# A decoder block on one core: B's transposes behind four tiles of h, pole operations earlier, the S5 input matrix two chunks later

## What is computed

```python
h = rmsnorm(x, norm1_g) * (1.0 + sc1) + sh1        # sh1, sc1, ...: silu(c) @ w_ada + b_ada
z = h @ w_in
u_conv, u_ssm, gl_conv, gl_ssm = split(z)
y_conv = silu(layernorm(causal depthwise conv of 31 taps over a * sigmoid(gate))) @ conv_proj
# S5: the poles give e = exp(dt * a); B is scaled by (e - 1) / a
bu = u_ssm @ B_bar;  x_t = e * x_{t-1} + bu_t;  y = C x + D u
y_ssm = za * sigmoid(zb),  where za, zb = split(gelu(y) @ w_glu)
x = x + g1 * ((sigmoid(gl_conv) * y_conv + sigmoid(gl_ssm) * y_ssm) @ w_out)
h = rmsnorm(x, norm2_g) * (1.0 + sc2) + sh2
x = x + g2 * ((silu(f_gate) * f_up) @ w_ffn_out);  out = rmsnorm(x, final_g)
```

## Time and profile before

| what | us |
|---|---|
| median of 3 runs | 2675.8 |
| lowest, highest | 2668.9, 2676.42 |
| profiled execution, its own time | 2679.86 |
| its span in the trace | 2678.1 |
| PE busy in the span | 2567.8 (96%) |
| DVE, POOL, ACT busy | 1504.9, 1821.0, 725.4 |

### The profile page before, as it was taken

The page is one execution under the profiler, slowest core; times in us unless marked ns, Lnnn a source line. Parts: engine busy times, 40 slices in busy tenths (PEclk is TensorE's granted clock), DMA queues, the critical chain, the costliest instruction groups (busy, mean ns, idle before and its releaser), DMA issues.

```text
span 2678.1 us, 30702 instructions
## 1 busy us (share of the span) xinstructions
PE 2567.8 (96%) x11675; PEld 2112.9 (79%) x11675; DVE 1504.9 (56%) x1782; ACT 725.4 (27%) x1120; POOL 1821.0 (68%) x1204
## 2 busy tenths in 40 slices
PE   6889999999999899989899999999999999999997
PEld 3778787878888788877788888878888878888886
DVE  4999733986299745987633334463333325544631
ACT  3212321133112321135333345443333322111100
POOL 2656675686776677665687777787777756666664
PEclk8999998999999999999999999999999999999999
DMA  8776347653765348562232232322323256655532
GB/s 266 183 183 187 112 162 153 173 184 103 213 169 183 114 145 203 151 204 87 94 103 87 81 116 73 112 84 71 95 71 95 73 196 205 196 163 181 173 134 71
DMA packets 420026, 378.29 MB, mean 141 GB/s; under 512 B 88024, under 2 KB 326312, under 8 KB 419752
## 3 DMA queue, kind: packets, MB, share of 16 engines
q1 hardware_dynamic: 321440, 299.48, 37.0%
q10 hardware_dynamic: 98440, 76.85, 10.3%
HBM read 312.11 MB, written 55.71 MB: 137 GB/s over the span
## 4 chain that ended last, share of the span: by engine, by line
PE 65%; DVE 25%; DMA 4%; issue 2%; ACT 2%; ACTq 1%; POOL 1%; DVEq 0%; POOLq 0%
PE bank L1546 13%; PE bank L1547 13%; PE bank L1548 13%; DVE bank L753 11%; PE bank L1777 6%; PE bank L1775 6%; PE bank L1776 6%; PE bank L1692 2%; PE bank L1694 2%; PE bank L1693 2%; DVE wst L809 1%; DVE bank L787 1%; DMA hraw<-hid_scratch 1%; DVE wst L789 1%; DMA u<-us_scratch 1%
## 5 line engine op out<-in xcount | busy, mean ns | idle before, releaser
L1845 POOL TENSOR_TENSOR w_lo<-raw,w_hi 128x1024 fp32r<-128x1024 f32 x192 | 484.0, 2521 | 15.4
L1843 POOL CAST w_hi<-raw 128x1024 fp32r<-128x1024 f32 x192 | 213.6, 1113 | 410.5 <-PE bank L1548 322.5
L1546 PE MATMUL bank<-h_hi,w_hi 128*128 128x512 f32 x896 | 354.6, 396 | 8.4 <-ACT sg_c L1185 6.5
L1547 PE MATMUL bank<-h_lo,w_hi 128*128 128x512 f32 x896 | 351.2, 392 | 0.0
L1548 PE MATMUL bank<-h_hi,w_lo 128*128 128x512 f32 x896 | 351.0, 392 | 0.0
L753 DVE SCALAR_TENSOR_TENSOR bank<-uc,cwt,bank 128x512 f32<-128x512 f32 x464 | 328.4, 751 | 8.0
L1868 POOL TENSOR_TENSOR fw_lo<-fsum,fw_hi 128x512 fp32r<-128x512 f32 x176 | 234.0, 1331 | 106.9 <-ACT fw_hi L1336 106.9
L1546 PE MATMUL bank<-xc_hi_T,fw_hi 128*128 128x512 f32 x704 | 276.6, 393 | 8.7 <-DVE tr L937 6.3
L1775 PE MATMUL bank<-ow_hi,hid_hi 128*128 128x512 f32 x704 | 274.7, 390 | 3.6 <-DVE hid_lo L997 3.6
L1548 PE MATMUL bank<-xc_hi_T,fw_lo 128*128 128x512 f32 x704 | 275.1, 391 | 0.0
L1547 PE MATMUL bank<-xc_lo_T,fw_hi 128*128 128x512 f32 x704 | 275.0, 391 | 0.0
(11 more groups left out here) (301 smaller groups left out, 5163.4 us busy)
## 6 DMA issues: line engine op xcount, KB each, us to landing
raw<-in_w_in SPq DMA_DIRECT2D x112, 512.0 KB, 4.7
raw<-in_w_ffn_in SPq DMA_DIRECT2D x66, 512.0 KB, 5.3
raw<-in_w_ffn_out SPq DMA_DIRECT2D x66, 512.0 KB, 4.5
hid_scratch<-tr SPq DMA_DIRECT2D x88, 256.0 KB, 2.5
hraw<-hid_scratch SPq DMA_DIRECT2D x88, 256.0 KB, 3.8
g2b<-in_w_ada SPq DMA_DIRECT2D x64, 256.0 KB, 4.2
ssm_m<-vk_scratch SPq DMA_DIRECT2D x32, 512.0 KB, 4.8
raw<-in_ssm_glu SPq DMA_DIRECT2D x32, 512.0 KB, 3.5
```

Source lines behind the costliest of these rows:

```text
L1546: t.matmul(dst, wh, xh, start=first, stop=False)
L1547: t.matmul(dst, wh, xl, start=False, stop=False)
L1843: g.tensor_copy(hi[:], src[:]).then_inc(hi_done, 1)
L1845: g.tensor_tensor(lo[:], src[:], hi[:].bitcast(F32), ALU.subtract).then_inc(split_done, 1)
```

## The change

Four edits. Nothing is computed in another way, and no instruction is added or dropped.

1. `nat_b` moves to the buffers tr and dt_, and B's 32 transposes move from between `ada1` and `ada3` to behind the transposes of h tile 3.
2. On DVE the first pole operations (L622 to L625 before) and the reduction of `th` move ahead of the wait for PE's `sums`; splits 0 to 4 of h come in a row, then `angles`, then splits 5 to 7.
3. PE's and ACT's `state_matrix` moves behind ug1. DVE does u0 and u1 together, and u2 after four output matrices.
4. ACT issues two kernel stores ahead of each of the four second exchanges, and does gl0 and gl1 ahead of the third and the fourth.

```diff
-        nat_b = early(h_at, tr_at, ...)
+        nat_b = early(tr_at, tr_at + 16384, ...)
...
-                names += conv_in(0) + [f"wt{n}" for n in R(8)] + ["ct0", "ct1"] + conv_in(1, 2, 3)
+                names += conv_in(0, 1) + [f"wt{n}" for n in R(8)] + ["ct0", "ct1"] + conv_in(2, 3)
...
+            dve.wait_ge(*scal.after("pro", "dt"))
+            link(v.tensor_tensor(lg, dt, ar, ALU.mult))
+            link(v.tensor_tensor(jexp[:], ...))
+            link(v.tensor_tensor(th, dt, ai, ALU.mult))
+            reduce_angle(th, th, t0)
             dve.wait_ge(*tensor.after("pro", "sums"))
             link(v.tensor_copy(modrow[:], bank[7][0:4, :]), "modrow")
...
             scale_of(0)
-            dve.wait_ge(*scal.after("pro", "dt"))
-            link(v.tensor_tensor(lg, dt, ar, ALU.mult))
-            link(v.tensor_tensor(jexp[:], ...))
-            link(v.tensor_tensor(th, dt, ai, ALU.mult))
-            h_split("pro", 0)
-            reduce_angle(th, th, t0)
-            h_split("pro", 1)
-            h_split("pro", 2)
+            for k in R(5):
+                h_split("pro", k)
             angles(jarg[:, 0, :, :], jarg[:, 1, :, :], jtmp[:], th, T + 1, "jargs")
-            for k in R(3, KD):
+            for k in R(5, KD):
                 h_split("pro", k)
...
             gated(0, 0)
+            gated(0, 1)
...
             for j in R(4):
                 output_matrix(j)
-            gated(0, 1)
+            gated(0, 2)
             for j in R(4, T + 1):
                 output_matrix(j)
-            gated(0, 2)
...
                 if b == 0:
                     sigmoid_u(0)
+                    sigmoid_u(1)
                     state_matrix()
                     rotation_tables()
...
-                if b == 0:
-                    store_kernel()
-                else:
+                if b:
                     sigmoid_u(2)
+                early_gates = 0 if b else 2
                 for q in R(NQ):
+                    if b == 0:
+                        store_kernel(2 * q, 2 * q + 1)
                     if b and q == 2:
                         sigmoid_u(3)
+                    if b == 0 and q >= 2:
+                        gate(q - 2)
                     act.wait_ge(*vec.after(b, f"sc{q}"))
                     exchange(dt_[q][:], wst[:, q * GQ:(q + 1) * GQ, 0:NC], turned_in[q])
                 act.wait_ge(*vec.after(b, "last"))
                 exchange(ctmp[:], carry[:], carry_in)
-                for i in R(GY[b]):
+                for i in R(early_gates, GY[b]):
                     gate(i)
...
             modulation_rows(1)
-            pe.wait_ge(bx_in, 64)
-            (32 transposes of nat_b, step "bx")
             modulation_rows(3)
...
-            for k in R(KD):
+            for k in R(4):
+                transposes("pro", k)
+            pe.wait_ge(bx_in, 64)
+            (32 transposes of nat_b, step "bx")
+            for k in R(4, KD):
                 transposes("pro", k)
...
                 if b == 0:
-                    conv_input(0)
+                    conv_input(0, 1)
                     state_matrix()
-                    conv_input(1, 2, 3)
+                    conv_input(2, 3)
                     kernel_tiles()
```

More of the change, by code:

```diff
@@ L267, in build @@
             ("iota_f", [P, NC + 1]), ("cx", [P, 2, 4, P]))
-        nat_b = early(h_at, tr_at, ("nat_b0", [G, 2, NST, HG]), ("nat_b1", [G, 2, NST, HG]))
+        nat_b = early(tr_at, tr_at + 16384, ("nat_b0", [G, 2, NST, HG]), ("nat_b1", [G, 2, NST, HG]))
         vm, = early(ync_at, mc_at, ("vm", [P, G, T + 1, HG]))
@@ L331, in pe_steps @@
             return names
-        pe_pro = ["v1", "ada1", "bx", "ada3", "v0", "ada5", "ada7", "sums", "mt"] + h_steps + ["v2"]
+        pe_pro = ["v1", "ada1", "ada3", "v0", "ada5", "ada7", "sums", "mt"] + h_steps[0:4] + ["bx"] + h_steps[4:] + ["v2"]
         pe_mix = [pe_steps(b) for b in R(NB)]
@@ L339, in act_steps @@
             if b == 0:
-                names += ["ug0"] + [f"wt{n}" for n in R(8)] + ["sk", "ck"] + [f"ug{m}" for m in R(1, KC)]
+                names += ["ug0", "ug1"] + [f"wt{n}" for n in R(8)] + ["sk", "ck", "ug2", "ug3"]
                 names += [f"kk{n}" for n in R(8)] + [f"S{q}" for q in R(NQ)]
@@ L613, in _ @@
             qr, qi, nr, den = (sv[:, n, :] for n in R(8, 12))
+            dve.wait_ge(*scal.after("pro", "dt"))
+            link(v.tensor_tensor(lg, dt, ar, ALU.mult))
+            link(v.tensor_tensor(jexp[:], iota_f[:, 0:T + 1].unsqueeze(2).broadcast_to([P, T + 1, G]),
+                                 lg.unsqueeze(1).broadcast_to([P, T + 1, G]), ALU.mult))
+            link(v.tensor_tensor(th, dt, ai, ALU.mult))
+            reduce_angle(th, th, t0)
             dve.wait_ge(*tensor.after("pro", "sums"))
@@ L1117, in kernel_tiles, with store_kernel @@
                         .then_inc(*scal.step(0, f"kk{n}"))
-            def store_kernel():
+            def store_kernel(*steps):
                 act.wait_ge(pro_v, mark["kst"])
                 act.wait_ge(zeros_in, 16)
-                for t in R(T):
+                for t in steps:
                     act.dma_start(vk_d[t * HG:(t + 1) * HG, :, 1, t * HG:],
@@ L1164, in mixers @@
                     sigmoid_u(0)
+                    sigmoid_u(1)
                     state_matrix()
                     rotation_tables()
-                    for m in R(1, KC):
-                        sigmoid_u(m)
+                    sigmoid_u(2)
+                    sigmoid_u(3)
                     kernel_tiles()
@@ L1512, in transposes @@
                 ins.then_inc(*tensor.step(stage, f"h{k}"))
-            for k in R(KD):
+            for k in R(4):
+                transposes("pro", k)
+            pe.wait_ge(bx_in, 64)
+            for n in R(2):
+                turned = bank[4 + n][:].rearrange("p (g h) -> p g h", h=HG)
+                for h in R(HG):
+                    ins = t.transpose(turned[:, :, h], nat_b[n][:, :, :, h].rearrange("g a p -> g (a p)"),
+                                      ident[0:G, 0:G])
+            ins.then_inc(*tensor.step("pro", "bx"))
+            for k in R(4, KD):
                 transposes("pro", k)
```

2 lines of the change are left out of this document (removed).

## The result

| | before | changed |
|---|---|---|
| median, us | 2679.5 (9 runs) | 2691.2 (9 runs, 2685.8 to 2692.7) |
| profiled execution, its time | 2679.86 | 2691.32 |
| its span | 2678.1 | 2689.5 |

The ratio is 1.0040, 95% interval 1.0023 to 1.0057: slower by 0.4%, with an interval clear of no change. The forecast was 2681.4 with a range up to 2689. Nine runs of the kernel before now have a median of 2679.5, where the prediction stood on three with 2675.8.

A forecast was written before the change was run, and what follows sets the result against it. The prediction took DVE to bound the changed stretch, almost without a gap from about 61.7 to 272 us. Its terms, -3.3 + 7.6 + 1.3 = +5.6 us on a median of 2675.8, gave 2681.4, range 2670 to 2689.

The forecast's parts named there:

- B's transposes: Start of block 0: slab 3's matmuls start earlier, so slab 7 lands sooner; -3.3 us, bounds -2.5 and -4.3.
- Pole operations: DVE around scale and the poles: little was on the path and later operations go at POOL's pace; 0.
- Kargs: Small operations and kargs on DVE, now beside POOL's chunks 8 and 9: +7.6 us, bounds +4.1 and 0.
- The walk: Operation-by-operation count of DVE's waits for POOL in the kargs stretch: sum 7.9 us, less 0.3 idle anyway, +7.6.
- The rival in which POOL pays in DVE's stead: In kargs the waits fall on POOL, which has time; 2672.5 to 2677, middle 2674 us; chance 0.23.
- ug2: After u0, ua2 starts at a low clock, so DVE waits for ug2's sigmoid; +1.3 us, up to +2.4.
- Scan: Block 0's scan, with kernel tiles and S0 to S3 on TensorE beside DVE's taps: 0.
- Stores and gates, turn back: ACT's spread stores and early gates fit between scans, and POOL has no split in DVE's turn back: 0.
- the rivals, at 0.13 and at 5 us: POOL's splits of chunks 18 and 19 fall into DVE's turn back; +5.6 + 5, about 2687 us; chance 0.13.
- a turn back over 13 us: Sign in block 0 that POOL's splits fall into DVE's turn back, which took 10.85 us before.
- the wait at 272: TensorE's 7.1 us wait for DVE's split of ys at the mixer's end, taking up the 6.5 us saved earlier.
- Sum: All terms together: -3.3 + 7.6 + 1.3 = +5.6 us, from the median 2675.8 to 2681.4.

The follow-up runs named there:

- e_poles: The kernel before with only the early pole operations, th reduction and reordered splits of h; u0 0.4 us later, no difference in time.
- e_hold: The changed kernel with POOL's split of chunk 8 in block 0 held until DVE's kargs is done; kargs stretch 14.60 us, block 1 3.5 us sooner.
- e_pieces89: The changed kernel with POOL's modulation pieces of chunks 8 and 9 put behind chunk 12; kargs stretch 20.18 us, block 1 0.2 us sooner.
- gates alone: The kernel before with gl0 and gl1 ahead of ACT's third and fourth exchange, stores in one row; turn 18.99 us, block 1 at 405.5.
- both: The kernel before with stores in pairs and gl0 and gl1 early; turn 15.93 us, block 1 at 401.6, no difference in time told.
- e_gates_late: The changed kernel with gl0 and gl1 behind all exchanges again, stores still in pairs; 2686.6 us, turn 14.21.
- e_fix: The kernel before with the changed prologue, POOL's pieces moved off poles and kargs, chunk 8's split held until kargs is done; 2668.9 us, ratio 0.9973.
- e_prologue: The kernel before with the moved B transposes and the early pole operations; two series, 2673.3 us against 2678.9 and 2673.6 against 2678.7.

## Why the prediction was wrong, step by step

- **B's transposes, -3.3.** Right. Slab 3's matmuls began at 22.50 and took 5.04 us, slab 7 landed at 33.64, 3.9 us sooner, scale was done at 42.73. The bounds were the clock's, and other executions with this edit lie between them or just below: the first small operation of kargs came 2.3 to 3.8 us sooner.
- **Pole operations, 0.** Right (`e_poles`: u0 +0.4, time the same). In the changed kernel the reduction of th met the split of chunk 0 and TensorE waited 1.9 us for modrow; scale was done 3.8 us sooner all the same.
- **Kargs, +7.6.** Right: 22.17 - 14.59 = 7.58, and 6.9 in the second execution. The walk was right not only in its sum. Operation by operation DVE lost 0.77, 2.08, 1.03, 0.72, 2.05 and 0.94 us, where the walk had nothing, 2.1, 1.25, 0.9, 2.4 and 1.28; taking all of POOL away took everything. The Trainium skill, SBUF — State Buffer, section "Who interferes with whom", has it that a DVE instruction with two SBUF inputs or in a 2-port mode and a GpSimd instruction that reads SBUF exclude each other for the whole instruction; the rows at 96.17 and 104.07 and `e_hold` agree. The rival in which POOL pays in DVE's stead fell: POOL's three rows from 100.28 on were 3.4 us longer as well, but DVE paid its 7.6.
- **ug2, +1.3.** 1.67 in the changed kernel, 1.5 in its second execution, up to 2.8 in others. What the prediction did not say is that this wait stands ready to take back what kargs gives (`e_hold`, `e_pieces89`).
- **Scan, 0.** 26.98 against 26.64.
- **Stores and gates, turn back, 0.** This is the step that failed: the turn back was 3.06 us longer, 3.05 to the first tap. The sentence was "POOL has no split to do in DVE's turn back". The parts were seen rightly: the early gates take away TensorE's stop that had kept POOL out (gates alone: turn 18.99 instead of 13.56), and the late load of chunk 18 had to keep it out in their place (both: 15.93). But I had that load landing near 198, and the turn back ends there as well: a margin of nothing, from a length of SP's loads that I took from no row. The split began at 195.80, some 2.5 us before the 198.4 at which an undisturbed turn back would have ended. The mechanism stood among the rivals, at 0.13 and at 5 us, and by the prediction's own sign, a turn back over 13 us, it is the one that holds. It came at 3 us, since chunk 18's split fell in whole but of chunk 19's only the start. That removing the gates' change gives back 2.4 us of the turn (`e_gates_late`) confirms it. The wait of 6.5 us which went "into the wait at 272" was not neutral.
- **Sum.** Block 0 came out at +8.5, 5.6 of it forecast; the 2.9 left are about the turn back's 3.06. The greater part of the miss is elsewhere. The point stood on a median of three runs, 2675.8, where larger series give 2678.1 to 2679.5. The profiled execution, 2679.86, would have given 2685.5, closer, but that was luck: profiled executions of other kernels here lie up to 7.5 us off their medians. And the first series was some 3 us slower than block 0 explains, which by its median a second one didn't repeat. What these 3 us were is open. With 3.7 for the base, 2.9 for block 0 and 3.2 for the series the miss of 9.8 us is covered.

## What to carry to other kernels

An engine that is on the critical path, and whose operations another engine can hold up as POOL does DVE's here, is protected by that other engine's waits. Before a wait of a third engine (here TensorE at gl4 and ahead of the state matrix) is removed, look up what it holds back, and what runs on the bound engine when that is let go. Put DVE work like kargs, which reads only SBUF, where POOL waits for loads or banks, or hold POOL's next piece with an explicit wait, as `e_hold` and `e_fix` do; but look for the next consumer first, since in `e_hold` holding a split for 15 us made ug2 late. And take as base of a forecast enough runs: the median of three was 3.7 us under that of nine, and a single profiled execution can be further off (`e_fix`: 2662.5 against a median of 2668.9).

## What the runs showed that I had not expected

- A DVE operation on 32 columns took 0.19 us or 2.33 us, by whether an instruction of POOL's split began just ahead of it. One such operation at the end of the carry moved a whole block by 2.1 us between two executions of one kernel.
- TensorE after 7.0 us of waiting: 4.5 us at a mean granted clock of 0.68. After 2.5 us: 1.00. The same matmuls behind it took 1.6 us more, by DVE's idle time until they were done (6.25 us in the kernel before, 4.63 in `e_prologue`). So the bound engine's delay can cost more than itself, and a gain there can bring more. The length of the wait alone does not tell which comes: in the kernel before, a wait of 2.39 us that ended at 1331.10 was followed by a granted clock of 0.50.
- An exchange of 2 times 128 KB took 8.1 us with some 2.5 MB of loads of SP issued just ahead of it, against 2.8 us in the median; in the kernel before the same exchange took 6.7 us beside such loads.
